# A diffusion block kernel: the first modulation weights loaded in two halves of the channels, and k of the first five tiles computed in two halves of the contraction

## The reference, cut to what matters

```python
mod_x = jax.nn.silu(c) @ w_ada[l] + b_ada[l]          # 6 x 1024 columns
mod_c = jax.nn.silu(c_ctx) @ w_ada[l] + b_ada[l]
sh1, sc1, g1, sh2, sc2, g2 = jnp.split(mod_x[:, None, :], N_MOD, axis=-1)
h_x = _modulate(_rms_norm(x, norm1_gain[l]), sh1, sc1)     # h * (1 + scale) + shift
h_c = _modulate(_rms_norm(ctx, norm1_gain[l]), csh1, csc1)
u, q, k, v, g, ga, gb = jnp.split(h_x @ w_in, list(IN_SPLITS), axis=-1)
q = _apply_rope(_to_heads(q), cos, sin)
k = _apply_rope(_to_heads(k), cos, sin) * scale
```

## Time and profile before

| | |
|---|---|
| median of 3 runs | 1307.93 us (1307.86 to 1310.1) |
| span of the profiled execution | 1306.3 us |
| PE busy | 1278.7 us, 98% of the span |
| share of the last chain that is PE | 93% |
| VectorE, ScalarE, GpSimd busy | 875.5, 605.1, 147.0 us |

### The profile page before, as it was taken

How to read it: one execution, slowest core, us unless ns; L and a number is a source line. 1 busy time by engine, 2 the same in 40 slices (tenths; PEclk the granted TensorE clock), 3 DMA queues, 4 the chain that set the end, 5 groups by cost and what they waited for, 6 DMA issues and landing times.

```text
span 1306.3 us, 16741 instructions
## 1 busy us (share of the span) xinstructions
PE 1278.7 (98%) x6140; PEld 1044.1 (80%) x6140; DVE 875.5 (67%) x1397; ACT 605.1 (46%) x1039; POOL 147.0 (11%) x87
## 2 busy tenths in 40 slices
PE   5999999999999999999999999999999999999997
PEld 1788788888888778888788888888888888888886
DVE  3563577752556987768588766556646568868866
ACT  6871221242123544452668655545555433554444
POOL 0216330102231000014530000000000000000000
PEclk8999999999999999999999999999999999999999
DMA  9414220202256455567852544444438986468634
GB/s 382 154 33 146 81 97 1 65 13 66 65 191 219 146 193 202 182 252 278 297 185 73 191 155 161 137 149 162 151 114 281 316 281 222 162 215 266 192 100 162
DMA packets 95098, 220.09 MB, mean 168 GB/s; under 512 B 12436, under 2 KB 12692, under 8 KB 93992
## 3 DMA queue, kind: packets, MB, share of 16 engines
q1 hardware_dynamic: 83184, 189.58, 42.8%
q10 hardware_dynamic: 10040, 23.15, 4.9%
q0 software_dynamic: 1792, 6.29, 1.4%
HBM read 167.59 MB, written 51.40 MB: 168 GB/s over the span
## 4 chain that ended last, share of the span: by engine, by line
PE 93%; DVE 3%; DMA 2%; issue 1%; ACT 1%; POOL 0%; SPq 0%; ACTq 0%; DVEq 0%
PE ps L2726 16%; PE ps L2728 15%; PE ps L2727 15%; PE ps L3266 8%; PE ps L3274 8%; PE ps L3269 8%; PE ps L3109 4%; PE ps L3104 4%; PE ps L3106 4%; PE ps L3292 3%; PE ps L2804 2%; DMA ada_in<-in_w_ada 2%; PE ps L2930 1%; PE ps L2912 1%; PE ps L2871 1%
## 5 line engine op out<-in xcount | busy, mean ns | idle before, releaser
L1005 POOL TENSOR_TENSOR ring_lo<-raw,ring_hi 128x1024 fp32r<-128x1024 f32 x42 | 102.7, 2458 | 500.4 <-ACT ring_hi L1088 500.3
L2726 PE MATMUL ps<-t_hi,s_hi 128*128 128x512 f32 x392 | 153.1, 391 | 0.0
L2728 PE MATMUL ps<-t_hi,s_lo 128*128 128x512 f32 x392 | 153.1, 391 | 0.0
L2727 PE MATMUL ps<-t_lo,s_hi 128*128 128x512 f32 x392 | 153.1, 390 | 0.0
L1646 ACT ACTIVATE s_hi<-s_raw 128x512 fp32r<-128x512 f32 x112 | 70.5, 630 | 115.2 <-DMA b<-in_w_stream 58.1
L2605 DVE TENSOR_TENSOR s_lo<-s_raw,s_hi 128x512 fp32r<-128x512 f32 x112 | 77.3, 690 | 44.5 <-ACT s_hi L1646 44.0
L2726 PE MATMUL ps<-ring_hi,hT_hi 128*128 128x512 f32 x232 | 94.2, 406 | 0.0
L2728 PE MATMUL ps<-ring_hi,hT_lo 128*128 128x512 f32 x232 | 90.7, 391 | 0.0
L2727 PE MATMUL ps<-ring_lo,hT_hi 128*128 128x512 f32 x232 | 90.5, 390 | 0.0
L2726 PEld LDWEIGHTS ps<-t_hi,s_hi 128*128 128x128 f32 x392 | 73.6, 188 | 16.2 <-DVE t_lo L2609 0.4
L2727 PEld LDWEIGHTS ps<-t_lo,s_hi 128*128 128x128 f32 x392 | 73.6, 188 | 15.9
(11 more groups left out here) (474 smaller groups left out, 3151.6 us busy)
## 6 DMA issues: line engine op xcount, KB each, us to landing
s_raw<-ff_scr SPq DMA_DIRECT2D x112, 256.0 KB, 2.9
raw<-in_w_stream SPq DMA_DIRECT2D x34, 512.0 KB, 4.3
ff_scr<-ffs SPq DMA_DIRECT2D x16, 1024.0 KB, 4.8
t_raw<-in_w_stream SPq DMA_DIRECT2D x64, 256.0 KB, 3.5
w_B_raw<-in_w_stream SPq DMA_DIRECT2D x48, 256.0 KB, 2.8
ff_scr<-ffa SPq DMA_DIRECT2D x16, 768.0 KB, 4.5
b<-in_w_stream SPq DMA_DIRECT2D x48, 256.0 KB, 4.3
ada_in<-in_w_ada SPq DMA_DIRECT2D x8, 1024.0 KB, 14.9
```

Source lines behind the costliest of these rows:

```text
L1005: nc.gpsimd.tensor_tensor(lo_ap, raw_of(i), hi_ap.bitcast(F32), ALU.subtract).then_inc(split, 1)
L2726: M(dst, lhsT=l_hi, rhs=r_hi, start=first, stop=False, skip_group_check=goes_on)
L2727: M(dst, lhsT=l_hi, rhs=r_lo, start=False, stop=False, skip_group_check=goes_on)
L2728: return M(dst, lhsT=l_lo, rhs=r_hi, start=False, stop=last, skip_group_check=goes_on)
```

## The change

w_ada's first 2048 columns are repacked outside the kernel into `ada_stream`: first the channels 0 to 511 of shift and scale (8 parts of 0.5 MiB, to `ada_a`), then the channels 512 to 1023 (to `ada_b`). The first half's rows are turned into `mod` and `a1` of four channel blocks, and with them k of the first five tiles (`EARLY`) begins over the first half of the contraction, each tile in a bank of its own (`K_BANK`). Parts of the second half's matmuls stand between. Then the five tiles get their second halves. The five later tiles are as before, but keys are transposed in bank 4 and one place later in the order, and ScalarE's copies of them too (`copy_kt`). Both contexts and tile 2, 3 load before the second half, and no tile is loaded by ScalarE. The decay masks are made in one exponential of 1024 columns, with the final product on VectorE behind the fifth tile's first half. The core of the diff:

```diff
+EARLY = 5
+SIDE = [("x", _s, 0) for _s in range(EARLY)] + [("x", _s, 1) for _s in range(EARLY)]
+SIDE += [("x", _s, _h) for _s in range(EARLY, 10) for _h in range(2)]
+K_BANK = {2: 5, 3: 6, 4: 7, 5: 0, 6: 1, 7: 5, 8: 6, 9: 7}
...
             load_x(sp, 0)
+            load_x(sp, 1)
+            for kt in range(KT):
+                sp.dma_start(ada_a[:, kt, :], ins["ada_stream"][0, kt]).then_inc(ht_landed[kt], 16)
             for i, (kind, n) in enumerate(STREAM):
+                if i == 2:
+                    load_x(sp, 2)
+                    load_x(sp, 3)
                     for kt in range(KT):
+                        sp.dma_start(ada_b_part(kt), ins["ada_stream"][1, kt]).then_inc(ada_b_in[kt], 16)
+                        if kt == 4:
+                            load_x(sp, 4)
...
+            first_hi(4)
             hi_to(("k", 3))
+            modulate(1)
+            second_hi(0)
+            second_hi(1)
...
+            for s in range(6, 14):
...
                 if s == 8:
                     hi_to(("v", 1))
                 if s == 11:
                     hi_to(("v", 3))
                 if s == 12:
                     hi_to(("q", 1))
-                if s >= 5:
-                    t = s - 5
-                    act.wait_ge(kt_done, t + 1)
-                    A(kT[:, :, t * P:(t + 1) * P], ps[:, 6, :].rearrange("p (a j) -> p a j", a=PAIRS), ACT.Copy
-                      ).then_inc(kt_free, 1)
+                copy_kt(s - 6)
...
+            modulate(4, 0)
+            first_lo(4)
+            dve.wait_ge(decay_exp, 4)
+            do.chain(V.tensor_tensor(dmask[:], dmask[:], head_wide(dist[:, 2, :]), ALU.mult))
+            mod_columns(1)
...
+            for kt in range(KT):
+                ada_part(0, kt)
+            pe.wait_ge(first_in, 16 * 3)
+            row_transposes(0)
+            x_transposes(0, (0,))
+            x_transposes(1, (0,))
+            k_part(0, 0, ("hh", "lh"))
+            k_part(1, 0, ("hh", "lh"))
+            x_transposes(2, (0,))
+            k_part(0, 0, ("hl",))
+            k_part(1, 0, ("hl",))
+            for kt in range(3):
+                ada_part(1, kt)
+            k_part(2, 0, ("hh", "lh", "hl"), lambda: x_transposes(3, (0,)))
+            for kt in range(3, 6):
+                ada_part(1, kt)
+            k_part(3, 0, ("hh", "lh"), lambda: x_transposes(4, (0,)))
+            for kt in range(6, KT):
+                ada_part(1, kt)
+            x_transposes(0, (1,))
+            k_part(4, 0, ("hh",))
+            row_transposes(1)
+            k_part(4, 0, ("lh", "hl"))
+            k_part(3, 0, ("hl",))
+            x_transposes(1, (1,))
+            for n in range(EARLY):
+                k_part(n, 1, ("hh", "lh", "hl"), lambda: x_transposes(n + 2, (1,) if n < 3 else (0, 1)) if n < 4 else None)
+            k_transposes(0)
+            x_transposes(6)
+            for s in range(EARLY, 10):
+                main(("k", TILES[s]), (lambda: k_transposes(4)) if s == 8 else None)
+                k_transposes(s - 4 if s < 8 else s - 3)
+                if s + 2 < 10:
                     x_transposes(s + 2)
```

More of the change, by code:

```diff
@@ L687, in side_bank @@
         def side_bank(key):
-            return (6 if key[:2] == ("x", 1) else 2) + SIDX[key] % 2
+            return 2 + SIDX[key] % 2
         def h_tile(t):
@@ L1822, in _ @@
                              dec[:, 0, :].rearrange("p (d a e) -> p e a d", d=2, e=2)))
-            def mask(h):
-                dve.wait_ge(decay_exp, 3 + 2 * (h + 1))
-                do(V.tensor_tensor(dmask[:, h, :], dtmp[:, h % 2, 0, :], dist[:, 2, :], ALU.mult))
-                do.chain(V.tensor_tensor(dtmp[:, h % 2, 2, :], dtmp[:, h % 2, 1, :], dist[:, 3, :], ALU.mult), decay_log)
-                do.chain(V.tensor_tensor(dmask[:, h, :], dmask[:, h, :], dtmp[:, h % 2, 2, :], ALU.add))
-            for h in range(HEADS):
-                mask(h)
             dve.wait_ge(first_in, 16 * 3)
@@ L2805, in transposes, with x_transposes @@
                 tr.then_inc(side_done, 1)
-            def x_transposes(s):
+            def x_transposes(s, halves=(0, 1)):
                 pe.wait_ge(xhat, s + 1)
-                for half in range(2):
+                for half in halves:
                     transposes(("x", s, half), [x_tile(s)[:, (4 * half + q) * P:(4 * half + q + 1) * P]
@@ new lines, in ada_part @@
+            def ada_part(hb, kt):
+                pe.wait_ge((ada_b_in if hb else ht_landed)[kt], 16)
+                src = ada_b_part(kt) if hb else ada_a[:, kt, :]
+                if hb and kt == 0:
+                    pe.wait_ge(rows_done, 1)
+                for q in range(4):
+                    mm = M(ps[32 * q:32 * q + 32, 4, 0:256], lhsT=silu_p[:, kt, :], rhs=src[:, q * 256:(q + 1) * 256],
+                           start=(kt == 0), stop=(kt == KT - 1))
+                if kt == KT - 1:
+                    mm.then_inc(ada_done, 1)
@@ new lines, in row_transposes, with k_transposes @@
+            def row_transposes(hb):
+                pe.wait_ge(rows_done, hb + 1)
+                for c in range(2):
+                    tr = nc.tensor.transpose(ps[:, 4, 256 + c * P:256 + (c + 1) * P], mod_rows[:, c * P:(c + 1) * P],
+                                             ident[:])
+                tr.then_inc(modT_done, 1)
+            def k_transposes(t):
+                main_read(pe, MIDX[("k", t)])
+                if t:
+                    pe.wait_ge(kt_free, t)
+                else:
+                    pe.wait_ge(mod_ready, 4)
+                for q in range(4):
+                    tr = nc.tensor.transpose(ps[:, 4, q * P:(q + 1) * P], kv[:, t, q * P:(q + 1) * P], ident[:])
+                tr.then_inc(kt_done, 1)
@@ L3416, in layouts @@
         "w_ada": a["w_ada"][0], "b_ada": b_ada,
+        "ada_stream": a["w_ada"][0][:, :2 * D].reshape(KT, P, 2, 2, 512).transpose(3, 0, 1, 2, 4).reshape(2, KT, P, D),
         "bmod1": col(b_ada[0, :2 * D]),
```

423 lines of the change are left out of this document (231 added, 192 removed).

## The result

The changed kernel takes 1310.47 us (median of 12 runs, 1307.81 to 1312.03) against 1307.93 us before (12 runs, 1307.03 to 1310.1): ratio 1.0019, 95% interval 1.0010 to 1.0027. Repeated in a second session it was 1310.31 against 1307.96, ratio 1.0021 (1.0012 to 1.0030). One of the 35 executions of the kernel before in that session took 1617.3 us, at a granted clock of 0.75, and is in neither ratio. The changed kernel is 2.4 to 2.5 us slower, at the edge of what I called no change, and within the range forecast; the forecast was 1309.2.

A forecast was written before the change was run, and what follows sets the result against it. PE bounds the kernel, behind a start of some 41 us. v at 99.3 against 101.24 gains 1.9, wait 5 takes 1.85, low clock adds 1.3: span 1307.6, median 1.6 above, 1309.2 us; range 1304.6 to 1311.6.

The forecast's parts named there:

- last part of the first half met: Start of the kernel: the last half-MiB part of the first half of w_ada lands and is met at 17.7 us.
- first k matmul: After copy, transposes, modulation and rounding of the first half, PE starts k at 22.2 us.
- wait for the remainder (and x_a): Just after k's start, PE waits some 0.4 us for the remainder, behind the second tile's modulation on VectorE.
- PE's own work to v: From k's start to v: matmuls, tile and key transposes, half parts, second rows and restarts, together 70.3 us.
- wait 1: Second rows' transposes wait 1.3 us for VectorE, which has the mask product ahead of the copy.
- wait 2: PE waits 2.25 us for ScalarE's rounding of tile 0's second half, behind the modulation of tile 1's second half.
- wait 3: The first key transposes wait 1.55 us for the turn (rope) on VectorE.
- wait 4: Key tile 5's transposes, behind k of tile 8, wait 1.3 us: VectorE's chain 14.9 us, PE's work 13.6.
- low clock behind the first k matmul: PE at half speed from 22.2 to 25.6 us: 1.7 lost, less 0.4 of waiting, so 1.3.
- wait 5: Behind v's start, key tile 7's transposes wait 1.85 us for a copy behind the rounding of q chunk 1.
- The rival that forecast them away: Rival, chance 24%: the three waits on key transposes, 4.7 us, are not met, giving 1304.5 us.
- some eight more restarts at 0.08: Part of PE's work before v: extra restarts of matmul runs, 0.6 us together.

The follow-up runs named there:

- first profile: Profile of the changed kernel's first profiled execution, nothing edited: 1307.81 us (span 1306.0), the shortest of its 12 runs.
- repeated: The changed kernel measured and profiled again, nothing edited: median 1310.31 us; the profiled execution took 1310.49 us (span 1308.7).
- experiment 6: Changed kernel with the four order edits of experiments 2, 3, 4 and 5 together, measured twice: 1302.57 and 1303.09 us, ratio 0.9961 both times against the kernel before.
- experiment 2: Changed kernel with ScalarE's copy of key tile 6 put back ahead of the rounding of q chunk 1: 1308.95 us, ratio 1.0005 against the kernel before.
- experiment 4: Changed kernel with key transposes and their copies one place later, q chunk 1 rounded behind key tile 6's copy: 1306.16 us, ratio 0.9987 against the kernel before.
- experiment 3: Changed kernel with ScalarE rounding the first tile's second half ahead of modulating the second tile's: 1309.97 us, ratio 1.0011 against the kernel before.
- experiment 5: Changed kernel with VectorE's final decay-mask product moved behind the last turn (rope) of k: 1309.27 us, ratio 1.0016 against the kernel before.
- experiment 7: Changed kernel without the early start, all 16 modulation parts run before the first k matmul: 1326.54 us, ratio 1.0148 against the kernel before.

## Why the forecast came out near

Point by point against the terms of the prediction, in us. The forecast took the low clock, so its column has the 1.3 in v:

| step | forecast | first profile | repeated |
|---|---|---|---|
| last part of the first half met | 17.7 | 18.25 | 17.90 |
| first k matmul | 22.2 | 22.57 | 23.33 |
| wait for the remainder (and x_a) | 0.4 | 0.69 + 0.48 | 0.18 |
| PE's own work to v | 70.3 | 72.4 | 72.4 |
| waits 1, 2, 3, 4 | 1.3, 2.25, 1.55, 1.3 | 0.99, 2.11, 1.61, 0.63 | 0.99, 2.11, 1.66, 0.60 |
| low clock behind the first k matmul | 1.3 net | 0 | 1.3 |
| v starts | 100.6 | 101.49 | 102.53 |
| wait 5 | 1.85 | 1.19 | 1.59 |
| span | 1307.6 | 1306.0 | 1308.7 |

PE's own work is v less the first k matmul, less the waits and the clock: 101.49 - 22.57 - 6.51, and 102.53 - 23.33 - 5.54 - 1.3.

- **The waits were there**, all five at the places named. The table has the idle times of the list, 5.3 for the first four against 6.4. The prediction reckoned a wait from where PE could have gone on, and so reckoned each is 0.16 to 0.25 longer (experiment 6): 1.16, 2.36, 1.77 and 0.79 in the first profile, 6.1 against 6.4. Only the fourth was well off, by 0.5: its chain of seven VectorE and ScalarE terms carries the errors of all. That they are on the path experiments 2, 4 and 6 show by the times, 3 and 5 by PE's rows only; that they add, experiment 6. The rival that forecast them away, 1304.5, is out.
- **PE's work was under-sized.** Of the 2.1 in the table 1.1 is that extra of six waits, and 1.0 is work. Key tiles were priced at 0.35 each; where the transposes of a tile follow they take 0.43 to 0.49, 0.5 more in all, and the kernel before has 0.44 at such a place too (67.72 to 68.16), so that this could have been read ahead. The matmuls took 1.1 more than 55.7 + 0.6. The step is "some eight more restarts at 0.08": their number was about right (20 runs of matmuls start behind something else, where the forecast had 18 in all), their price was not. In the rows from 50.19 to 52.12 four matmuls take 1.01 behind transposes and 0.92 otherwise, so a start costs 0.1; k's first eight matmuls lost 0.4 (22.57 to 24.82), and those that run into a modulation part 0.1 each time. Modulation and tile transposes took 0.5 less than forecast.
- **The clock was right for most profiles and wrong for the first, and its size came out by luck.** The low level ended at 27.4 us and not at 25.6. The forecast's 1.3 was net, 1.7 less a wait of 0.4. The measured 1.3 is not net: the waits for the remainder and for `x_a` shrank with it from 1.17 to 0.18, so behind k's start the low level cost 79.20 - 78.92 = 0.3. Most of its cost lies ahead of that, where the forecast had none: the transposes take 1.92 against 1.04, and from the last part to the first matmul it is 5.43 us against 4.32. This is why k started at 23.33 and not at 22.2.
- **Wait 5** was 0.1 to 0.5 too long (1.75 and 1.35 in the prediction's reckoning), since q chunk 1 was rounded 5.6 and 5.2 us behind v's start and not 5.8.
- **The sum.** Where PE goes on behind key tile 7, the repeated run stands 110.24 - 107.17 = 3.1 us behind the kernel before, and the forecast had it 1.3 behind. PE's last matmul starts 1301.26 - 1298.41 = 2.85 behind, and the ends are 1308.7 - 1306.3 = 2.4 apart: what follows PE's last matmul took 0.45 less, and no run here says why. In the first profile the 1.6 of key tile 7 is down to 0.7 by 444 us (444.33 against 443.60), because PE doesn't meet there the wait that the kernel before has at `g_B_lo`; the repeated run has it too, 0.7 long. Gains do pass through that place: the first profile of experiment 6 is 5.9 us ahead of the kernel before in front of it and 6.5 behind it, and 6.7 at the end.

So the mechanism was right: the early start was worth its time, five waits stood at the places named, and a low clock came with it. That the number came within 1.3 us of the median is in part luck. In the repeated run k's start was 1.1 late and PE's work 1.1 longer than forecast, waits 1 to 4 were 0.3 and wait 5 was 0.1 shorter, and 0.7 of what remained was not there at the end.

One phrase of the prediction misreads the rows: no transposes of 0.35 stand between 101.24 and 106.81, and the 5.57 us are 24 matmuls and one start. And the terms shown for wait 4 don't give its 14.9 us: 6.6 and VectorE's five make 14.7, and 16.6 with the two v chunks. It measured 0.5 less than forecast.

**Where the 11 us went.** k started 34.21 - 23.33 = 10.9 us earlier in the repeated run, yet v 1.3 later; from first k matmul to v it was 67.0 us before and 79.2 after, 12.2 more. Of this the moved modulation matmuls are 4.05 (in the first profile 30.70 to 32.13, 35.54 to 36.97, 39.47 to 40.47, and the rows' two transposes at 0.19), the waits 5.5, the low clock, which before had ended by k's start, 1.3. The remaining 1.3, and the 1.4 of waits in that stretch that before had and after has not, make 2.7. Of these, 0.8 are eight transposes: the kernel before had both context tiles transposed whole ahead of k's start (16 transposes), the changed one only their first halves. Some 0.6 are the uncounted 0.16 to 0.25 of five waits against two, and the last 1.3 are restarts. These are sums of rows; no run took them out one by one. Experiment 7 shows the other side: without the early start v would come some 11.5 us later, by the estimate there. Experiment 6 shows that what the waits took can be had back by order alone.

## What to carry to other kernels

Where the bound engine is given work earlier, its neighbours' orders must move with it. Here three of the five waits (1, 2 and 5) were one instruction standing ahead of another that the bound engine wanted first, two (3 and 4) were rows of the bound engine placed before their data could be there, and four edits of order turned 2.4 us lost into 5 us gained. Count what cutting does to the bound engine: each piece of an accumulation that starts behind a transpose cost 0.1 us, and each wait 0.2 us more than the list of waits shows. When an early start is taken out to price it, compare the waits and the clock as well: here the edit put in 4.5 us of its own. And before a trace is explained, look where its execution stands among the runs; here the profiled one was the fastest of 12, and a second profile differed from it by 2.7 us at three places, of which the clock at the start explains one.

## What the runs showed of the hardware

- PE's level in the first 30 us differs between executions of the same kernel: full from about 17 us in one and low until 27.4 in the other, with the same work. Of ten profiles of kernels with the early start and no added matmuls, eight met k's first matmuls at the low level and two at the full one. It lasted until 29.9 us in experiment 6. v came 1.0 and 2.9 us later for it (0.5 of the 2.9 is a later transfer). PE had run parts of 1.08 us every 1.28 us at the time, and stood for 0.6 to 1.3 us at the hand-overs.
- Behind a wait of 2.1 us the granted clock fell for 3.4 us in three profiles (experiments 2, 3 and 7) and not in seven others with such a wait.
- A VectorE remainder from and to SBUF took 0.69 us alone. Begun while GpSimd was at its own remainder it took 1.73 and 2.42, and it ended 0.56 and 0.55 us behind GpSimd's, as if it had stood until GpSimd was through. One that began together with GpSimd's took 0.69, and GpSimd's took 3.02 in place of 2.36.
